# Head 0's scores, the square sums and the reciprocal root moved in front of an expert gather with one more row buffer

## The reference

```python
def peer_ffn(x, w_q, sub_keys, u, v):        # x is the normed stream, 256 x 1024
    q = (xb @ w_q).reshape(128, 8, 2, 128)                        # 8 heads, 2 halves
    scores = jnp.einsum('thpd,hpkd->thpk', q, sub_keys)           # 128 keys per half
    top_s, top_i = lax.top_k(scores, 16)
    cand_s = top_s[:, :, 0, :, None] + top_s[:, :, 1, None, :]    # 16 x 16 candidates
    best_s, best_pos = lax.top_k(cand_s, 16)
    expert = jnp.take_along_axis(cand_i, best_pos, axis=-1)       # of 16384 experts
    gate = jax.nn.softmax(best_s, axis=-1)
    act = jax.nn.gelu(jnp.einsum('thkd,td->thk', u[expert], xb))
    return jnp.einsum('thk,thkd->td', gate * act, v[expert])
```

## Time and profile before

| | |
|---|---|
| time, median of 3 runs | 2067.52 us (2064.16 to 2068.56) |
| the profiled execution: its time, its span | 2070.1 us, 2068.3 us |
| PE, DVE, ACT, POOL busy | 90%, 63%, 44%, 16% of the span |
| moved from memory | 482.21 MB read, mean 236 GB/s |
| first instruction of unit pq 0 on PE | 1373.70 us |
| first gather issued | 1400.42 us |
| last gather's dot product | 2060.68 us |

### The profile page before, as it was taken

One profiled execution on the slowest core, in us unless ns is written; L12 is line 12 of the kernel. 1 busy time (PEld: TensorE's weight loads), 2 busy tenths in 40 slices (PEclk: granted clock), 3 DMA queues, 4 the chain that ended last, 5 costly groups with the idle time before them and its releaser, 6 DMA issues.

```text
span 2068.3 us, 29845 instructions
## 1 busy us (share of the span) xinstructions
PE 1864.9 (90%) x11656; PEld 1498.1 (72%) x11656; DVE 1306.1 (63%) x2383; ACT 919.1 (44%) x1876; POOL 329.7 (16%) x346
## 2 busy tenths in 40 slices
PE   7999899999999999999999888899987777877777
PEld 7999879999999999869999878788332222232222
DVE  5555775555655552686555765565977777676444
ACT  4444464444444431474444443544544443444343
POOL 1000101000100010001000000053533333333331
PEclk9999999999999987999999899999999999999999
DMA  7555427955455534204555243257999999999997
GB/s 271 184 183 176 135 67 140 318 184 184 153 184 186 187 118 144 82 26 159 183 185 187 77 143 103 93 172 272 422 421 421 422 421 421 422 421 421 421 421 312
DMA packets 96971, 488.35 MB, mean 236 GB/s; under 512 B 10640, under 2 KB 10896, under 8 KB 63808
## 3 DMA queue, kind: packets, MB, share of 16 engines
q0 software_dynamic: 38368, 274.74, 34.5%
q1 hardware_dynamic: 58464, 211.70, 30.4%
HBM read 482.21 MB, written 4.19 MB: 235 GB/s over the span
## 4 chain that ended last, share of the span: by engine, by line
PE 59%; DMA 24%; DVE 11%; ACT 4%; issue 2%; POOL 0%; SPq 0%; ACTq 0%; POOLq 0%; DVEq 0%
DMA YL<-uv,A 22%; PE PS L492 16%; PE PS L494 16%; PE PS L493 16%; PE PS L2020 2%; DVE WL L930 2%; DMA XF<-uv,A 1%; PE PS L1503 1%; DVE YL L1472 1%; DVE A L1225 1%; DVE A L1011 1%; PE PS L1750 1%; DVE XL L941 1%; ACT WH L602 1%; DVE small L1024 1%
## 5 line engine op out<-in xcount | busy, mean ns | idle before, releaser
L492 PE MATMUL PS<-XH,WH 128*128 128x256 f32 x2176 | 631.1, 290 | 39.8 <-DVE WL L930 16.1
L494 PE MATMUL PS<-XH,WL 128*128 128x256 f32 x2176 | 622.0, 286 | 0.0
L493 PE MATMUL PS<-XL,WH 128*128 128x256 f32 x2176 | 621.9, 286 | 0.0
L930 DVE TENSOR_TENSOR WL<-raw,WH 128x1024 fp32r<-128x1024 f32 (+1 forms) x377 | 444.0, 1219 | 88.5 <-ACT WH L602 87.8
L492 PEld LDWEIGHTS PS<-XH,WH 128*128 128x128 f32 x2176 | 420.9, 193 | 47.7 <-issue 32.8
L602 ACT ACTIVATE WH<-raw 128x1024 fp32r<-128x1024 f32 (+1 forms) x390 | 386.9, 1041 | 95.2 <-PE PS L494 69.6
L493 PEld LDWEIGHTS PS<-XL,WH 128*128 128x128 f32 x2176 | 421.7, 194 | 0.2
L494 PEld LDWEIGHTS PS<-XH,WL 128*128 128x128 f32 x2176 | 421.1, 194 | 0.0
L884 ACT ACTIVATE A<-A,RTK 128x1 f32<-128x1 f32 x256 | 75.3, 294 | 333.0 <-DVE A L1472 330.9
L540 POOL TENSOR_TENSOR A<-hT 128x256 f32<-128x256 f32 x64 | 56.3, 906 | 954.5 <-DVE hT L974 732.4
L492 PE MATMUL PS<-GH,WH 128*128 128x256 f32 x704 | 198.1, 281 | 0.0
(11 more groups left out here) (303 smaller groups left out, 2670.7 us busy)
## 6 DMA issues: line engine op xcount, KB each, us to landing
raw<-wst SPq DMA_DIRECT2D x388, 512.0 KB, 4.4
raw<-wst SPq DMA_DIRECT2D x9, 384.0 KB, 3.2
vscr<-A POOLq DMA_DIRECT2D x1, 3072.0 KB, 36.0
A<-vscr POOLq DMA_DIRECT2D x1, 2048.0 KB, 22.2
C<-cst SPq DMA_DIRECT2D x1, 1236.5 KB, 11.1
raw<-uv,A POOLq DMA_INDIRECT x72, 30.1
hT<-xin SPq DMA_DIRECT2D x2, 512.0 KB, 5.4
A<-vscr POOLq DMA_DIRECT2D x1, 1024.0 KB, 12.1
```

Of the source, the lines that this page charges most:

```text
L492: pe.matmul(o, wh, xh, start=start, stop=False, skip_group_check=True)
L493: pe.matmul(o, wh, xl, start=False, stop=False, skip_group_check=True)
L494: return pe.matmul(o, wl, xh, start=False, stop=stop, skip_group_check=True)
L930: dv.tensor_tensor(WL[:, m % SPL, 0:w], raw[:, i % RAW, 0:w], f32(WH[:, m % SPL, 0:w]), ALU.subtract).then_inc(s_lo, 1)
```

## The change

Five things change, all in the PEER layer.

1. POOL makes no low halves any more (it made those of pq 3 to 8, ON_POOL). DVE makes pq 3 and 4 before it routes head 0, and pq 5 to 15 behind it, with the steps of head 1 between them.
2. On PE the square sums move from behind pq 0 to behind pq 1 and head 0's scores, and `by_token(7)` from behind pq 1 to behind pq 3. On ACT `root(7)` moves behind head 0's score copies. On DVE `rstd(7)` and `by_token(2)` move behind head 0's routing.
3. QP holds six query units in place of 16 (QN_RING), so ACT's copy of unit n waits for the scores of head (n - 6) // 2. The freed arena holds one more row buffer, ROW1, free from the start, so SLOTS is 15.
4. ACT takes the first softmax exponentials behind unit 13 in place of behind unit 15.
5. The residual stream is added to block 0's banks just before g = 0 and to block 1's before g = 32; the output tiles OT move onto hT.

```diff
-ON_POOL = (3, 9)
-SLOTS = 14
+SLOTS = 15
+QN_RING = 6
...
+        ROW1 = view(pr, 2048)
+        QP = view(pr, QN_RING * T, QN_RING, T)
+        DG = view(pr, 512, 4, 128)
...
-        rows = [..., (ROW0, [(s_sbp, 4)]),
+        rows = [..., (ROW0, [(s_sbp, 4)]), (ROW1, []),
...
 POOL, behind squares(7):
-            for m in range(POOL0, POOL1):
-                i = spl_unit[m]
-                po.wait_ge(s_hi, m + 1)
-                po.tensor_tensor(WL[:, m % SPL, :], raw[:, i % RAW, :], f32(WH[:, m % SPL, :]), ALU.subtract).then_inc(s_lop, 1)
...
 ACT:
             prenorm(7)
+            hi("pq", 0)
             for kc in range(8):
                 ins = ac.activation(XF[:, kc, :], ...)
...
             for n in range(16):
                 hi("pq", n)
-                if n == 0:
-                    root(7)
                 ac.wait_ge(s_used, U("pq", n))
-                ac.activation(QP[:, n, :], PS[:, n % 2, 0:T], ACT.Copy).then_inc(s_qp, 1)
+                if n >= QN_RING:
+                    ac.wait_ge(s_scm, (n - QN_RING) // 2 + 1)
+                ac.activation(QP[:, n % QN_RING, :], PS[:, n % 2, 0:T], ACT.Copy).then_inc(s_qp, 1)
                 for h in scored(n):
                     ...
-            shares(0, 0, 2)
+                if n == 1:
+                    root(7)
+                if n == 13:
+                    shares(0, 0, 2)
...
 DVE:
             prenorm(7)
-            rstd(7)
-            by_token(2)
+            lo("pq", 1)
...
             for k in range(6):
                 route(0, 0, k)
-            for n in range(ON_POOL[1], 16):
+            rstd(7)
+            by_token(2)
+            for n in range(5, 16):
                 ...                                      # low half of pq n
-                if n - ON_POOL[1] < 6:
-                    route(0, 1, n - ON_POOL[1])
-            shares(0, 0, 2)
+                if 6 <= n < 12:
+                    route(0, 1, n - 6)
+                if n == 12:
+                    shares(0, 0, 2)
             gates(0, 0, 2)
...
 PE, in the loop over pq:
-                if n == 0:
-                    sums(7)
                 if n == 1:
-                    by_token(7)
                     pe.wait_ge(s_sk, 16)
                 if n == 3:
+                    by_token(7)
                     pe.wait_ge(s_txf, 1)
                     pe.wait_ge(s_rtk, 3)
                     ...                                  # the 16 transposes of XF
                 for h in scored(n):
                     ...
+                if n == 1:
+                    sums(7)
```

More of the change, by code:

```diff
@@ L442, in program @@
         PQ0 = split[where["pq"][0]]
[L443 to L449, removed]
         def U(name, n):
@@ L482, in program @@
             last[i % RAW] = split[i]
-        rows = [(flat(YH[:, :, :]), [(s_used, U("upab", 7))]), (flat(YL[:, :, :]), []), (ROW0, [(s_sbp, 4)]),
+        rows = [(flat(YH[:, :, :]), [(s_used, U("upab", 7))]), (flat(YL[:, :, :]), []), (ROW0, [(s_sbp, 4)]), (ROW1, []),
                 (flat(XF[:, :, :]), [(s_xtt, 4)])]
-        rows += [(flat(raw[:, 2 * k:2 * k + 2, :]), [low_done(last[2 * k]), low_done(last[2 * k + 1])])
+        rows += [(flat(raw[:, 2 * k:2 * k + 2, :]), [(s_lo, 1 + max(last[2 * k], last[2 * k + 1]))])
                  for k in sorted(range(4), key=lambda k: max(last[2 * k], last[2 * k + 1]))]
@@ L858, in act_program, with shares @@
             ins.then_inc(s_txf, 1)
+            def shares(blk, h0, n):
+                ac.wait_ge(s_bd, GATES[blk, h0])
+                bd = BD[:, h0:h0 + n, :]
+                ac.activation(bd, bd, ACT.Exp, scale=RTK[:, blk:blk + 1]).then_inc(s_bde, 1)
             for n in range(16):
                 hi("pq", n)
-                if n == 0:
-                    root(7)
                 ac.wait_ge(s_used, U("pq", n))
-                ac.activation(QP[:, n, :], PS[:, n % 2, 0:T], ACT.Copy).then_inc(s_qp, 1)
+                if n >= QN_RING:
+                    ac.wait_ge(s_scm, (n - QN_RING) // 2 + 1)
+                ac.activation(QP[:, n % QN_RING, :], PS[:, n % 2, 0:T], ACT.Copy).then_inc(s_qp, 1)
                 for h in scored(n):
@@ L869, in act_program @@
                                       ACT.Copy).then_inc(s_scr, 1)
-            def shares(blk, h0, n):
-                ac.wait_ge(s_bd, GATES[blk, h0])
-                bd = BD[:, h0:h0 + n, :]
-                ac.activation(bd, bd, ACT.Exp, scale=RTK[:, blk:blk + 1]).then_inc(s_bde, 1)
-            shares(0, 0, 2)
+                if n == 1:
+                    root(7)
+                if n == 13:
+                    shares(0, 0, 2)
             for g in range(256):
@@ L1482, in weights @@
                 m = U(name, n) - 1
-                pe.wait_ge(*low_done(m))
+                pe.wait_ge(s_lo, m + 1)
                 return WH[:, m % SPL, :], WL[:, m % SPL, :]
@@ L2007, in pe_program @@
                     ins.then_inc(s_scm, 1)
-            for blk in range(2):
-                pe.wait_ge(*((s_qp, 16), (s_scr, 16))[blk])
-                for kc in range(8):
-                    pe.matmul(PS[:, YB[blk] + kc // 4, 128 * (kc % 4):128 * (kc % 4) + 128],
-                              hT[:, kc, 128 * blk:128 * blk + 128], c("ident"), start=kc % 4 == 0, stop=False,
-                              skip_group_check=True)
+                if n == 1:
+                    sums(7)
             for g in range(256):
                 blk, s = g // 128, g % 128
+                if g in (0, 32):
+                    yb = g // 32
+                    pe.wait_ge(*((s_qp, 16), (s_scr, 16))[yb])
+                    for kc in range(8):
+                        pe.matmul(PS[:, YB[yb] + kc // 4, 128 * (kc % 4):128 * (kc % 4) + 128],
+                                  hT[:, kc, 128 * yb:128 * yb + 128], c("ident"), start=kc % 4 == 0, stop=False,
+                                  skip_group_check=True)
                 pe.wait_ge(s_g[g % SLOTS], 16 * (g // SLOTS + 1))
```

11 lines of the change are left out of this document (4 added, 7 removed).

## The result

The changed kernel took 2073.61 us, the median of 22 runs (2066.36 to 2077.66); the kernel before took 2067.41 us in 22 runs (2063.84 to 2071.49). The ratio of the two is 1.0021, with a 95% interval of 1.0011 to 1.003. So the change makes the kernel some 4 us slower; whether that is more than 0.2% the interval leaves open. The profiled execution of the changed kernel took 2074.13 us with a span of 2072.3, against 2070.1 and 2068.3 before. By its own profiled execution the prediction said 2073.7.

What follows compares the result with a forecast made beforehand. Bound: when PE ends pq 15, freeing XH, then the remaining gathers on full DMA engines. +4.5 (later end) + 1.65 (clock) - 2.5 (row) = +3.6 us: 2073.7 profiled, 2071.1 against the median; range 2067 to 2074.5.

Steps and rivals of the forecast that it cites:

- The bound: Last third: the end is X + 0.3 us plus 2.53 us for each gather not home by then.
- One more row home: ROW1 lets nine gathers, not eight, be home by X, leaving 247: -2.5 us.
- First pause: PE waits ahead of head 0's scores for ACT's query copies, behind the XF copies: 1.7 us.
- Routing: Head 0's routing on DVE shrinks from 12.05 to 9.35 us, as POOL makes no low halves.
- Second pause: PE's turn to token order waits for the reciprocal behind head 0's routing; transposes at 1394.95, +4.46 us.
- X: The end of pq 15 on PE, which frees XH; claimed to move by +4.5 us.
- Cost of the clock: PE's clock falls behind the second pause, slowing transposes and pq 4: 1.65 us, bounds 0 and 6.6.
- The row at 1437.1: Trace of the kernel before: 3.1 us PE rest with clock staying 1.00; no-fall rival +2.0 us, chance 0.25.
- Gather 0 earlier: POOL issues the first gather at 1393.1 instead of 1400.42; claimed worth nothing while DMA runs dry before X.
- The rival in which that, or a ring 15 deep, pays: Gathers: 15 buffers move more than 14, -42 us, near 2029; or earlier first gather, -7.3 us; chance 0.07.
- The sum: Whole kernel: +4.5 (X) + 1.65 (clock) - 2.5 (a row) = +3.6 us; chance 0.45.

Runs made afterwards that it cites:

- e6: Changed kernel with square sums, root, reciprocal and turn to token order behind pq 15, and ACT's XF copies behind head 0's score copies; 2062.22 us, ratio 0.9984.
- e1: Changed kernel with 14 row buffers, without ROW1; 2070.54 us, ratio to the kernel before 1.0019.
- e4: Kernel before in its own order, with only the ring of six query units, moved tiles and the 15th row buffer; 2062.62 us, ratio 0.9978.
- e2: Changed kernel with 20 extra unused products on PE ahead of the turn to token order; 2067.35 us, ratio to the kernel before 1.0001.
- e7: Changed kernel unaltered, run again with another set of runs of the kernel before; 2067.98 us, ratio 1.0023.
- e3: Changed kernel with the reciprocal between steps 1 and 2 of head 0's routing and PE's turn behind pq 2; 2064.38 us, ratio 0.9984.
- e8: Kernel of e6 with DVE's first six dot products ahead of the reciprocal and two small tiles exchanged; 2061.12 us, ratio to the kernel before 0.9961.
- e5: Kernel of e3 with ACT's eight XF copies moved behind head 0's score copies, ahead of the root; 2065.55 us, ratio to the kernel before 1.0005.
- e9: Kernel of e4 run once more, in the set of e8; 2063.88 us, ratio to the kernel before 0.9982.

## Why the prediction was right, and where it was off

**The bound.** That the end is the XH gather plus the transfer of what is not home held in all eleven profiles: from that gather to the end it is 633.3 to 633.8 us with 15 rows (634.4 in e6, where gather 15 waits for a late y product), and 635.7 and 636.2 with 14.

**One more row home: -2.5.** Measured -2.6 here, 2.1 (e1) to 2.9 (e4) elsewhere. The nine rows were home: 4 GB/s between 1436 and 1438.

**First pause: 1.7.** PE idled 1.39. The cause was as said, XF ahead of the copy of pq 1 on ACT.

**Routing: 9.35.** Measured 9.38; the two casts that took 2.37 and 0.68 take 0.18 each once POOL makes no low halves, and 2.37 and 0.69 again in e4, where it makes them. The Trainium skill (SBUF — State Buffer, SBUF: two separate sides) says that DVE and GpSimd share a pair of ports which one of them holds exclusively for a whole instruction, for operations of certain kinds; the trace agrees in that the cast grew beside POOL's low half and shrank with it gone, but no run isolated the port.

**Second pause, X at +4.5.** The two pauses together came to 4.35 us where the clock did not fall (e2, e7). The step was +4.46.

**Cost of the clock: 1.65.** This is the term that was mis-sized. There was a fall, as in the forecast, but in the profiled execution it lasted 6.8 us, from some 1393.2 to 1400.0, with PE at work for all but the 0.34 us ahead of the transposes, and the run without it (e2) puts its cost at 3.0 us. The second profile of the same kernel has 3.4 us of it at a cost of 1.7, so the forecast's figure holds for one execution and is little more than half of the other's. I had sized it from one short fall of 3.3 us behind a rest of 1.8; the long one of 13.2 us stood beside it in the earlier trace rows, and a value between them was nearer. The trace of the kernel before holds more to size it by: 19 stretches at 0.50 ahead of this stage, read in windows of 0.5 us, 13 of them some 3.5 us long, four some 7, one 14 and one 24. The row at 1437.1, which I took for a rest without a fall, is the rest itself and does not show what follows; behind it, from 1440.2 to 1443.0, the clock is at 1.00 as well. The Trainium skill (TensorE: Matmul & The Clock Gate, Part 1: The HAM clock gate) makes the clock follow how busy PE has been lately; e2, in which 20 useless products alone kept it at 1.00, agrees.

**Gather 0 earlier: nothing.** It went out at 1391.73, 1.4 earlier than forecast, and e3 has it 2.1 us later relative to pq 0 with the same way to the end. The rival in which that, or a ring 15 deep, pays is dead: the landings are 2.48 us apart with 14 and with 15 rows.

**The sum.** +4.76 + 2.61 - 2.6 = +4.8 us in the profiled execution with the start of pq 0 left out, against a predicted +3.6: 1.35 us more of clock, 0.1 less of pause and 0.1 more from the row. The XH gather at 1438.73 lies for the same reason just above the 1436.5 to 1438.5 of the forecast. That the profiled execution, at 2074.1, came within 0.4 of the predicted 2073.7 is in part luck: an early start of pq 0 hides 0.7 us of the error, and the second profiled execution took 2066.78. The median of the changed kernel is 6.2 above that of before, and the mean ratio is 4.3 us; the two differ because the changed kernel's 22 times lie in two groups (10 from 2066.4 to 2070.3, 12 from 2073.5 to 2077.7), so that its median falls at the edge of one. The spans of e7, 2065.0, and of the first profile, 2072.3, fit such groups. Of the 7.3 us between them 5.9 are the start of pq 0 and 1.3 the fall, so the drift of the start is the larger part; what makes the groups wasn't tried. My forecast of 2071.1 set the profiled execution 2.6 above the median of the runs; for the changed kernel it lies 0.5 above it, and that conversion is 2.1 of the 2.5 us by which the median lies above the forecast.

## What to carry to other kernels

Where buffers come free late, ask of each moved step whether it stands before or behind the release of the last one, not when the first transfer starts: here 8.7 us of earlier start were worth nothing, and 3.3 us less ahead of the release (e6, e8) gave 3.3 in the pieces, less 0.4 to 1.0 behind it. A short dependent step that is put behind a long serial chain of another engine can cost its wait twice, once as idle time and again as a lower clock on the dense work behind it (not each time: the rest of 1.21 us in e5 was followed by no slower turn or transposes); look in that chain for an earlier place, and check what the step that it displaces was hiding (e5). And where the start of a stage drifts by more than the effect, compare stage by stage between the same two instructions, and run the unaltered kernel a second time.

## What the runs showed that I had not expected

- The same rest in the same program is followed by falls of different length: 6.8 us at 0.50 in one execution, 3.4 us in another, at a cost of 3.0 and 1.7 us. In e1, with the same order on PE, pq 0 to XH was 65.77 as in the first. In e4 and e9, which are one program, a rest of 3.21 us ahead of the first y product is followed by no fall and by a fall; the product takes 1.95 and 3.63 us (rows below). There it costs next to nothing (633.3 and 633.5 us from XH to the end), with the DMA engines as the bound.
- A fall can be bought off: 20 products without use in a pause of 2.4 us took nothing and gave back 3.0 us, seven tenths of what the two pauses themselves cost.
- A ring one row shorter (e1) did not show in the ratio of whole runs (1.0019 against 1.0021), though it showed plainly, at 2.1 us, in the piece of the profile that it acts on.
- Single waits of an engine come out 2 to 3.4 us longer in one execution than the same wait in a like kernel, with nothing in the profile that ended them: ACT's at 1407.73 in e9, DVE's at 1436.92 in e8.

The first y product in PE's timeline of e4, then of e9:

```profile
1439.47 1.95 PE L2024 MATMUL PS<-YH,A 128*128 128x512 f32 x4 [3.21 <-ACT A L896]
...
1440.33 3.63 PE L2024 MATMUL PS<-YH,A 128*128 128x512 f32 x4 [3.21 <-issue]
```
